# One streaming-encoder kernel: u in three parts with a new product order, norms summed by matmul, and a pool stage that reads PSUM directly

## The reference

```
x = x + 0.5 * ((silu(a) * b) @ w_out)          # a, b = halves of rmsnorm(x) @ w_in, D_FF = 2816
pool: d = windowed_mean(u) - u;  y = (d @ w_pool + b_pool) * scale;  x = x + y   # u = rmsnorm(x)
      new_pool = last 15 rows of u
```

## Time and profile before

| | |
|---|---|
| median of 3 runs | 1986.25 us (1985.67 to 1988.85) |
| the profiled execution | 1983.19 us |
| its span | 1981.4 us |
| mean granted clock of PE | 0.972 |
| idle of PE ahead of 75 us | 41 us, in six gaps |
| idle of PE in all | 85 us |

### The profile page before, as it was taken

One profiled execution on the slowest core, in us unless ns is written; L12 is line 12 of the kernel. 1 busy time (PEld: TensorE's weight loads), 2 busy tenths in 40 slices (PEclk: granted clock), 3 DMA queues, 4 the chain that ended last, 5 costly groups with the idle time before them and its releaser, 6 DMA issues.

```text
span 1981.4 us, 34425 instructions
## 1 busy us (share of the span) xinstructions
PE 1896.3 (96%) x13880; PEld 1875.2 (95%) x13880; DVE 1267.0 (64%) x1920; ACT 852.2 (43%) x1478; POOL 390.9 (20%) x397
## 2 busy tenths in 40 slices
PE   3899999998999999999999999999999899999996
PEld 3899999998999999999999999999989899999996
DVE  6776377666876477687764776552446977447743
ACT  3553155435554155435541554232334455235521
POOL 6120022123321022132200221200001522012122
PEclk7899999997999999999999999999999999999997
DMA  4675377430675277427752773321112476357531
GB/s 120 153 158 128 80 174 160 122 91 19 146 163 130 79 171 161 125 73 165 156 136 76 172 165 84 94 92 58 65 43 99 89 170 156 101 119 169 127 89 62
DMA packets 115853, 234.70 MB, mean 118 GB/s; under 512 B 13232, under 2 KB 13248, under 8 KB 115696
## 3 DMA queue, kind: packets, MB, share of 16 engines
q1 hardware_dynamic: 76608, 160.89, 26.2%
q0 software_dynamic: 38208, 69.42, 22.0%
q10 hardware_dynamic: 880, 2.20, 0.3%
HBM read 228.92 MB, written 3.53 MB: 117 GB/s over the span
## 4 chain that ended last, share of the span: by engine, by line
PE 87%; DVE 7%; ACT 2%; DMA 2%; issue 1%; DVEq 0%; POOL 0%; SPq 0%; ACTq 0%
PE ps L1509 47%; PE ps L1499 36%; DVE w_lo L1050 1%; DVE u L1103 1%; DVE rstd L1109 1%; ACT w_hi L678 1%; DMA raw_x<-in_ffn_in 1%; DVE raw_z L1056 1%; PE ps L1783 0%; PE ps L1667 0%; DMA raw_y<-in_ffn_in 0%; ACT u L714 0%; DVE stage L1084 0%; DVE side L1094 0%; PE ps L1786 0%
## 5 line engine op out<-in xcount | busy, mean ns | idle before, releaser
L1509 PE MATMUL ps<-u,w_hi 128*128 128x288 f32 x4928 | 996.1, 298 | 52.5 <-ACT side L743 18.9
L1509 PEld LDWEIGHTS ps<-u,w_hi 128*128 128x128 f32 x4928 | 799.5, 190 | 57.0 <-issue 47.0
L1509 PE MATMUL ps<-u,w_lo 128*128 128x288 f32 x2464 | 732.8, 297 | 0.0
L1509 PEld LDWEIGHTS ps<-u,w_lo 128*128 128x128 f32 x2464 | 467.4, 190 | 0.0
L1499 PE MATMUL ps<-h_hi,w_lo 128*128 128x288 f32 x1408 | 302.7, 296 | 0.0
L1499 PE MATMUL ps<-h_lo,w_hi 128*128 128x288 f32 x1408 | 302.6, 296 | 0.0
L1499 PE MATMUL ps<-h_hi,w_hi 128*128 128x288 f32 x1408 | 302.6, 296 | 0.0
L678 ACT ACTIVATE w_hi<-w_raw 128x768 fp32r<-128x768 f32 (+3 forms) x164 | 137.2, 838 | 339.8 <-PE ps L1499 303.4
L1050 DVE TENSOR_TENSOR w_lo<-w_raw,w_hi 128x768 fp32r<-128x768 f32 (+3 forms) x164 | 174.1, 1062 | 155.8 <-ACT w_hi L678 155.2
L532 POOL DMA_DIRECT2D raw_y<-in_ffn_in x88 | 76.2, 877 | 803.9 <-DVE raw_z L1056 797.8
L1499 PEld LDWEIGHTS ps<-h_hi,w_hi 128*128 128x128 f32 x1408 | 226.5, 189 | 0.0
(11 more groups left out here) (222 smaller groups left out, 2188.3 us busy)
## 6 DMA issues: line engine op xcount, KB each, us to landing
raw_a<-in_ffn_in SPq DMA_DIRECT2D x176, 256.0 KB, 4.7
w_raw<-in_ffn_out SPq DMA_DIRECT2D x64, 384.0 KB, 3.1
raw_y<-in_ffn_in SPq DMA_DIRECT2D x88, 256.0 KB, 3.3
raw_x<-in_ffn_in SPq DMA_DIRECT2D x88, 256.0 KB, 2.7
raw_x<-in_ffn_in POOLq DMA_DIRECT2D x88, 256.0 KB, 6.2
raw_y<-in_ffn_in POOLq DMA_DIRECT2D x88, 256.0 KB, 4.9
raw_z<-in_ffn_in POOLq DMA_DIRECT2D x88, 256.0 KB, 4.5
w_raw<-in_ffn_out SPq DMA_DIRECT2D x64, 320.0 KB, 2.9
```

What stands on the lines that cost most here:

```text
L1509: mm = pe.matmul(dst, w, m, start=prod in ("M1", "M2", "M5") and kp == 0 and p == 0, stop=kp == KP - 1 and p == 2, skip_group_check=prod i ...
```

## The change

1. Order: M2 of pairs 0 and 1 come next to each other as products 5 and 6, then both M6, both M7, M4 and M3 of pair 0. The bank of M2 of pair 1 is 2; M1 of pair 2 waits for it.
2. u in three parts: pieces 0-1, 2-3, 4-6, each with its own semaphore. In the first half of each FFN PE takes M1 of both pairs, then M5 of both, then M2 (part 1), then the rest (part 2).
3. Norms of ffn_a and ffn_b: ACT squares each x tile into `sq8`, PE adds them with 16 f32 matmuls (`norm_tiles`) ahead of product 7, and POOL does no squares there. The norms of ffn_c and ffn_d stay as they are, ahead of product 5.
4. Pool norm and last norm: `last_square` moves ahead in `ffn_out`, DVE adds it to `sumsq`, and PE needs half the column matmuls.
5. Pool stage: DVE adds the bias to x first (8 tensor_scalar), then adds scale times PSUM straight to x; two stages alternate; windows come earlier in PE's order; POOL makes the state with the gains first and the norm later.
6. Start: ACT's queue loads gains and x tiles 0, 2, 4, SP both A11 first.

```diff
-    order = [("M1", 0), ("M5", 0), ("M1", 1), ("M5", 1), ("M6", 0), ("M2", 0), ("M7", 0), ("M2", 1),
-             ("M6", 1), ("M4", 0), ("M3", 0), ("M7", 1)]
+    order = [("M1", 0), ("M1", 1), ("M5", 0), ("M5", 1), ("M2", 0), ("M2", 1), ("M6", 0), ("M6", 1),
+             ("M7", 0), ("M7", 1), ("M4", 0), ("M3", 0)]
...
-ROOT_AT = (9, 4, 4, 4)
+NORM_AT = (6, 6, 4, 4)
+ROOT_DONE_AT = (8, 8, 5, 5)
+PARTS = ((0, 2), (2, 4), (4, 7))
...
+    def q_bank(n):
+        return ps[:, 2 if n == 1 else 5, 0:HALF]
...
+            def u7_high(f, kp, part):
+                if part == 1:
+                    act.activation(u7[:, kp, 0, 2:4, :], halves(x[:, 2 * kp + 1, :]), ACT.Copy,
+                                   scale=ngains[:, f.norm, 2 * kp + 1:2 * kp + 2]).then_inc(u7_hi[1], 1)
+                    return
...
+            def square_tile(j):
+                act.activation(sq8[:, j, :], x[:, j, :], ACT.Square).then_inc(sq8_made, 1)
...
+            for j in (2, 4, 6):
+                square_tile(j)
+            first_odd(0)
+            first_odd(1)
+            u7_high(ffn_a, 0, 2)
+            first_odd(2)
+            u7_high(ffn_a, 1, 2)
+            first_odd(3)
+            upto(ffn_a.unit(0, "M2", 0))
...
+            def add_last(norm):
+                dve.wait_ge(sq_last, {N_POOL: 1, N_FINAL: 2}[norm])
+                dve.wait_ge(sumsq_ready, SUM_TURN[norm])
+                dve.tensor_tensor(sumsq[:, :], sumsq[:, :], sq[:, :], ALU.add).then_inc(sumsq_full, 1)
...
                 dve.wait_ge(unit_used, f.unit(ph, "M2", n) + 1)
+                if n < 2:
+                    dve.wait_ge(s1_copied, g + 1)
...
+            for j in range(DT):
+                last = dve.tensor_scalar(x[:, j, :], x[:, j, :], pool_bs[:, j:j + 1], None, ALU.add)
...
+                    dve.wait_ge(pool_psum, 3 * g + m + 1)
+                    dve.scalar_tensor_tensor(x[:, j, 0:SEQ], ps[:, 6 + m, :], vecs[:, 1, j:j + 1], x[:, j, 0:SEQ],
+                                             ALU.mult, ALU.add)
...
+            pool_z(0)
...
+            pool_z(1)
+            pool_x(0)
+            pool_z(2)
+            pool_u(0)
+            pool_x(1)
+            pool_z(3)
+            pool_u(1)
+            for g in range(2, GROUPS):
+                pool_x(g)
+                pool_u(g)
...
+                if prod == "M1" and n == 2:
+                    pe.wait_ge(gate_first, g)
...
+            def norm_tiles(f):
+                for i, j in enumerate((0, 2, 4, 6, 1, 3, 5, 7) if f is ffn_a else range(DT)):
+                    pe.wait_ge(sq8_made, DT * f.i + i + 1)
+                    for h in range(2):
+                        mm = pe.matmul(ps[:, 6 + h, 0:HALF], mean_w[:, :], sq8[:, j, h * HALF:(h + 1) * HALF],
+                                       start=i == 0, stop=i == DT - 1)
...
+                    together = (ORDER[0:2], ORDER[2:4])
...
+                        if f in (ffn_a, ffn_b):
+                            norm_tiles(f)
+                        else:
+                            norm(f.norm)
...
             pool_project(0)
             norm_cols(N_POOL)
+            norm_hist()
             pool_project(1)
-            pool_project(2)
             pe.wait_ge(bands_landed, 16)
             pool_windows(0)
+            pool_project(2)
+            pool_windows(1)
             pool_project(3)
-            for g in range(1, GROUPS):
-                pool_windows(g)
+            pool_windows(2)
+            pool_windows(3)
```

More of the change, by code:

```diff
@@ L307, in encoder_step @@
     N_POOL_OUT = 2
+    SUM_TURN = {N_POOL: 1, 3: 2, N_MIX: 3, 5: 4, N_FINAL: 5}
     def stage(f, kp):
-        return stages[kp] if f in (ffn_a, ffn_d) else side
+        if f is ffn_b:
+            return side if kp % 2 else spare
+        return side if f is ffn_c else stages[kp]
     hist_hi, hist_lo, bands_landed = sem("hist_hi"), sem("hist_lo"), sem("bands_landed")
@@ L700, in negs_even @@
                 st = stage(f, kp)
[L701 to L702 removed]
+                if kp and f is ffn_c:
+                    act.wait_ge(u7_made[2], KP * f.i + kp)
+                elif kp >= 2 and f is ffn_b:
+                    act.wait_ge(u7_made[2], KP * f.i + kp - 1)
                 act.activation(st[:, 0, :], x[:, 2 * kp, 0:HALF], ACT.Copy,
@@ L791, in ffn_in, with ffn_out @@
                 h_high(f, ph, PAIRS - 1)
-            def ffn_out(f, ph, following=None, norm=None, dst=None):
+            def ffn_out(f, ph, following=None, norm=None, dst=None, square=None):
                 for j in range(DT):
                     ahead(f.unit(ph, "out", j, 0))
+                    if square is not None and j == DT - 1:
+                        last_square(square)
                     if following is not None or norm is not None:
@@ L994, in _ @@
                     negs_odd(ffn_d, j // 2)
+                if j == 1:
+                    for part in range(3):
+                        u7_high(ffn_d, 0, part)
             act.wait_ge(x_ready, 5 * DT + DT - 1)
@@ L1184, in ffn_in, with ffn_out @@
                 h_low(f, ph, PAIRS - 1)
-            def ffn_out(f, ph, following=None, norm=None, tiles=None, count=0):
+            def ffn_out(f, ph, following=None, norm=None, tiles=None, count=0, square=None):
                 for j in range(DT):
@@ L1202, in ffn_out @@
                             sums_even(following, j // 2)
+                    if square is not None and j == DT - 1:
+                        add_last(square)
+                        if norm is not None:
+                            u_low(j, norm, *tiles, count + j + 1)
+                        ahead(f.unit(ph, "out", j, 1))
+                        return
                     ahead(f.unit(ph, "out", j, 1))
                     if following is not None:
-                        u7_low(following, j // 2, j % 2)
+                        if j % 2:
+                            u7_low(following, j // 2, 1)
+                        u7_low(following, j // 2, 2 * (j % 2))
                     elif norm is not None:
@@ L1235, in _, with pool_z @@
                               ALU.subtract).then_inc(hist_lo, 1)
-            ffn_out(ffn_a, 1, norm=N_POOL, tiles=(up_hi, up_lo))
-            rstd_cols(N_POOL, 4 + 2 * HIST)
-            def pool_x(g):
-                for m in range(2):
-                    j = 2 * g + m
-                    dve.wait_ge(pool_y_ready, j + 1)
-                    if j == 0:
-                        dve.wait_ge(state_made, 1)
-                    dve.tensor_tensor(x[:, j, :], x[:, j, :], pool_y[:, m, :], ALU.add).then_inc(x_ready, 1)
-                sums_even(ffn_b, g)
-                sums_odd(ffn_b, g)
-                u7_low(ffn_b, g, 0)
-                u7_low(ffn_b, g, 1)
-                ahead(U_POOL + g)
-            for g in range(GROUPS):
+            ffn_out(ffn_a, 1, norm=N_POOL, tiles=(up_hi, up_lo), square=N_POOL)
+            dve.wait_ge(u_ready, DT)
+            dve.wait_ge(state_step, 2)
+            for j in range(DT):
+                last = dve.tensor_scalar(x[:, j, :], x[:, j, :], pool_bs[:, j:j + 1], None, ALU.add)
+            link(last)
+            rstd_cols(N_POOL, 4)
+            def pool_z(g):
                 dve.wait_ge(unit_used, U_POOL + g + 1)
@@ L1457, in _ @@
                 if j == 1:
-                    u7_low(ffn_d, 0, 0)
-                    u7_low(ffn_d, 0, 1)
+                    for part in range(3):
+                        u7_low(ffn_d, 0, part)
                 elif j == DT - 2:
@@ L1472, in _ @@
             ffn_in(ffn_d, 1)
-            ffn_out(ffn_d, 1)
+            ffn_out(ffn_d, 1, square=N_FINAL)
             rstd_cols(N_FINAL, 4)
```

325 lines of the change are left out of this document (181 added, 144 removed).

## The result

| | before | after |
|---|---|---|
| median | 1985.96 us (1983.27 to 1988.85, 4 runs) | 2006.42 us (2000.42 to 2008.50, 4 runs) |
| profiled execution, its span | 1983.19, 1981.4 us | 2000.42, 1998.6 us |
| mean granted clock of PE | 0.972 | 0.974 |

The changed kernel is slower: the ratio is 1.0101, with a 95% interval of 1.0080 to 1.0123. I had forecast 1994 with a range of 1964 to 2004. The direction was right; the time lies 2.4 us above the range.

The account below looks back on a forecast made before the run. PE, busy 96% of the span, was taken as the bound. Terms -8.8, +16, +5.6, +2.5, -4.0 and -1.3 made +10.0, taken as +8: 1983.19 to 1991, plus 3.1 for the median, 1994; range 1964 to 2004.

Parts of the forecast that it names:

- The second halves: Four FFN second halves: the new order makes PE stall for M2 of pair 1, +4.0 us each, +16 in all.
- The chain: Second half starting at T: A12 load, output tile, S4, M3, `gate_one` end at T+11.0 us; PE wants them at T+8.0.
- the clock term: Second halves: half clock behind each 3.0 us stall of PE, taken as 1.0 us on the mean.
- The start: Start and first half of ffn_a: M5 of pair 2 begins at 66.1 us, not 74.92, so -8.8 us.
- the last norm: End of kernel: a 2.51 us gap and 4.1 us of column matmuls become 0.76 and 2.0 us; -1.3 us.
- the stall for the first z of the pool stage: Pool stage: eight bias additions, 4.0 us on DVE, make z(0) late by some 3 us for PE.
- The sum of ffn_b: First half of ffn_b: M1 starts at 486, product 7 comes at 509; with the pool stage -4.0 us.
- ffn_c: First half: norm, `gate_one` and later waits cost +10.9 us, less old gaps 2.0 and 1.5 and half clock 1.7: +5.6.
- ffn_d: First half: the same chains as ffn_c give 11 to 12 us against old gaps of 8.4 with the clock: +2.5.
- The stalls stay hidden: Rival, whole kernel: A12 or S4 comes early, `gate_one` is ready before PE wants it; -28 us, 1958; chance 0.13.
- half hidden: Rival: chain costs 1 us a half without clock loss, ffn_c and ffn_d even; -10 us, 1976; chance 0.22.
- Slower than forecast: Rival: each new gap takes 1.7 us of clock, S4 lands at 5.5; 5.7 a half, ffn_c 8; 2004; chance 0.15.

Follow-up runs that it names:

- the wait: Changed kernel, but M2 of pair 1 no longer waits for `gate_one` of pair 0: 1987.88 us, ratio 1.0015 to the kernel before.
- the buffer: Changed kernel, but A12 of odd pairs gets its own buffer, with the wait for `gate_one` kept: 1989.73 us, ratio 1.0021 to the kernel before.
- the order: Changed kernel, but with the former order of the first twelve products in each FFN's second half: 1987.91 us, ratio 1.0014 to the kernel before.

## Why the prediction was right and wrong

**The second halves were right in their mechanism.** The chain was forecast at +16 and measured +16.0. The runs on the wait, the buffer and the order show these three links; S4's share is read from the traces alone. That the sum came out to a tenth is luck. In the first of the four A12 took 4.4 us from issue to ready where the earlier trace rows had 3.2, S4 4.1 where I took 4.5, and PE started M2 of pair 1 at T + 11.8 for T + 11.0, a gap of 3.7 for 3.0. The other three had gaps of 2.7 to 3.1, the mean is 3.1, and the clock term of 1.0 was 0.9 on the mean (3.4 us of half clock behind two of the gaps, none behind the two others). The start (-7.9 for -8.8) and the last norm (-2.1 for -1.3) hold, the latter by less than it seems. As written, 2.51 and 4.1 us that "become" 0.76 and 2.0 would be -3.8; the -1.3 needs the gap to stay, which it did (3.15), and the column matmuls took 1.3 and not 2.0.

**The step that failed is the stall for the first z of the pool stage:** its price. The prediction had the bias additions ahead of z and PE late "by some 3 us" for it, but no loss of clock behind that stall. The stall measured 3.68 us, and the half clock behind it 5.6 more, as the run with the bias later alone shows (9.3). By that the pool stage gained 6.4 us where 12.6 were forecast, and with ffn_b's first half the term was +1.05 for -4.0. Without the block it would have been -7.9. The eight additions were not the error: 4.0 us forecast, 3.52 measured. The Trainium skill, "VectorE: DVE Perf Modes", section "The perf-mode tier table", has an fp32 tensor_scalar in SBUF at twice the rate of a tensor_tensor, from which I had an estimate of 2.9 for the eight. At 0.44 us each for 576 columns, where a two-input step of that size takes 0.76, the trace agrees with the faster mode and lies 0.08 us an instruction above that estimate. The sum of ffn_b has a hole besides: six products, 0.6 and 7.7 behind 486 make 504, and the text has 509 without saying where the 5 us come from. Measured, ffn_b lost 7.4 for 8.6.

**In ffn_c the same thing was missed.** The gaps were of the forecast kind (the norm wait, then `gate_one`, then `up_two`) and not larger than forecast: 3.98, 3.34 and 1.85, or 9.2 us in all, for 10.9.

```profile
902.84 1.37 PE L1641 MATMUL ps<-sumsq,mean_w 128*128 128x288 f32 x4 [3.98 <-POOL sumsq L519]
910.42 0.63 PE L1606 MATMUL ps<-u,w_hi 128*128 128x288 f32 x2 [3.34 <-DVE tmp L1177]
922.01 0.50 PE L1606 MATMUL ps<-u,w_hi 128*128 128x288 f32 x2 [1.85 <-DVE side L1194]
```

```profile
904.00:907.00 3.00, 3.00 (x13) 0.50 0.30 26
911.00:914.00 3.00, 3.00 (x15) 0.50 1.05 332
```

But the sum took off 1.7 us for the half clock of the old gaps and put nothing in for that of the new ones, whose two stretches at 0.50 cost twice that. With it the gaps give 9.2 - 3.5 + 1.7 = +7.4 for the +7.2 measured, where +5.6 was forecast. In ffn_d the new gaps and their clock come to some 11.6 us, within the 11 to 12 that I gave them, 7.65 of it for `gate_one` alone; against the 8.4 of the old ones that makes +3.2. Why the half grew by 4.6 stays open; such a half differs by 1 to 2 us between profiles.

**The discount and the range.** The terms summed to +10.0 and I took +8, "since each chain was laid with every step at its full length". On the whole the chains took their full length; the 2 us were taken off on no row. The profiled executions differ by 17.2: 8 forecast, 2.0 for the discount, 5.05 for the pool stage with ffn_b, 3.7 for ffn_c and ffn_d, 0.9 for the start, less 2.4 for the last norm and the mLSTM. The median of after stands 6.0 above its profiled execution, where I had added the 3.1 of before: 2.9 us that no mechanism here explains, and without which the time would have stayed within the range. The range left out what the text had worked out: the bounds of the pool stage (to +4) and of ffn_c and ffn_d together (to +16) were not added to its top. They alone reach 8.0 and 7.9 us above their terms, which is 2010 from 1994.

**The rivals.** "The stalls stay hidden" and "half hidden" fell: all four gaps are there. "Slower than forecast" is what came, by the sum, but not by its mechanism, which was full clock loss and a slow S4 in every second half.

## What to carry to other kernels

Ask of every instruction that a change puts ahead of others on a queue who is the last to be fed from behind it, and look for waits in the middle of a stage's loop, not only at its start. Give each stall of PE a range for the slow clock behind it, here from nothing to 5.6 us behind one of 3.7, and do so in every stage of the sum, for new gaps as for old ones. When a new order lets two products of one kind follow each other, count their raw buffers first: one more buffer and one guard that was no longer needed turned this change from 1.0% slower into 0.6% faster.

## What the runs showed of the hardware

- A stall of PE of 3.68 us in the pool stage was followed by 12 us at a granted clock of 0.50, and taking it away gave back 9.3 us in all. Gaps of 2.7 to 3.7 us in the four second halves cost 0.9 us more than themselves on the mean: 2.0, -0.3, 1.7 and 0.2 in ffn_a to ffn_d. In this case the loss behind a gap was anything between none and more than the gap.
- The sixteen f32 matmuls of 288 columns took 7.92 us, in fp32r 2.28, a factor of 3.5.
- The same load of 256 KB took 3.2 us from issue to the first use in one kernel and 4.4 in the other, with the DMA engines equally busy (0.66 and 0.64).
- Stretches without any edit differ between profiles by up to 6 us (the mLSTM, 345.7 to 351.8; the first half of ffn_c by 3), more than most terms of such a sum.
